# w_down of a hybrid decoder layer in fp32: which output columns use seven products, and in what order ScalarE serves them

## What is computed

```
h = rmsnorm(x, ffn_norm)
gate, up = h @ w_gate, h @ w_up          # 2048 x 5632 each
x = x + (silu(gate) * up) @ w_down       # 5632 x 2048
out = rmsnorm(x, final_norm)
```

## Time and profile before

| | us |
|---|---|
| median of 3 runs (lowest, highest) | 1979.58 (1979.37, 1979.76) |
| span of the profiled execution | 1977.3 |
| its own time, one of the above, so | 2.1 to 2.5 above the span |
| TensorE busy | 1967.3 (99%) |
| VectorE busy | 1654.7 (84%) |
| ScalarE busy | 1126.6 (57%) |
| POOL busy | 167.2 (8%) |
| HBM read | 242.99 MB |

### The profile page before, as it was taken

One profiled execution on the slowest core, in us unless ns is written; L12 is line 12 of the kernel. 1 busy time (PEld: TensorE's weight loads), 2 busy tenths in 40 slices (PEclk: granted clock), 3 DMA queues, 4 the chain that ended last, 5 costly groups with the idle time before them and its releaser, 6 DMA issues.

```text
span 1977.3 us, 29282 instructions
## 1 busy us (share of the span) xinstructions
PE 1967.3 (99%) x10300; PEld 1691.6 (86%) x10300; DVE 1654.7 (84%) x2386; ACT 1126.6 (57%) x2064; POOL 167.2 (8%) x261
## 2 busy tenths in 40 slices
PE   9999999999999999999999999999999999999998
PEld 7888888888888988888888888888888888888886
DVE  8877767777766999999999999999998688697886
ACT  6566666666346655555646555555556355566643
POOL 5002333223100000000000000000000000000000
PEclk9999999999999999999999999999999999999999
DMA  9322222224334344443434344444347836546433
GB/s 343 127 83 70 70 71 70 69 70 139 102 117 138 119 148 137 130 139 130 137 132 142 131 134 135 136 139 135 132 138 238 303 120 227 176 148 221 126 130 133
DMA packets 132889, 276.16 MB, mean 140 GB/s; under 512 B 13392, under 2 KB 13424, under 8 KB 131744
## 3 DMA queue, kind: packets, MB, share of 16 engines
q1 hardware_dynamic: 120896, 239.65, 37.9%
q0 software_dynamic: 6640, 23.82, 3.1%
q10 hardware_dynamic: 5232, 11.04, 1.6%
HBM read 242.99 MB, written 31.46 MB: 139 GB/s over the span
## 4 chain that ended last, share of the span: by engine, by line
PE 96%; DVE 2%; issue 1%; DMA 1%; ACT 0%; SPq 0%; POOLq 0%; POOL 0%; DVEq 0%; ACTq 0%
PE bank L841 25%; PE bank L844 13%; PE bank L702 7%; PE bank L768 7%; PE bank L770 7%; PE bank L769 7%; PE bank L704 7%; PE bank L703 7%; PE bank L900 3%; PE bank L898 3%; PE bank L899 3%; PE bank L925 2%; PE bank L942 1%; PE bank L910 1%; PE bank L909 1%
## 5 line engine op out<-in xcount | busy, mean ns | idle before, releaser
L841 PE MATMUL bank<-s_two,t_hi 128*128 128x512 f32 x2352 | 557.3, 390 | 0.0
L1485 ACT ACTIVATE t_hi<-t_raw 128x1792 fp32r<-128x1792 f32 x176 | 302.5, 1720 | 358.1 <-DVE t_raw L2155 269.7
L841 PEld LDWEIGHTS bank<-s_two,t_hi 128*128 128x128 f32 x2352 | 433.5, 188 | 84.7
L2161 DVE TENSOR_TENSOR t_lo<-t_raw,t_hi 128x1792 fp32r<-128x1792 f32 x176 | 355.7, 2021 | 20.7 <-ACT t_hi L1485 20.6
L844 PEld LDWEIGHTS bank<-s_two,t_lo 128*128 128x128 f32 x2352 | 298.9, 191 | 10.4 <-DVE t_lo L2161 0.6
L844 PE MATMUL bank<-s_two,t_lo 128*128 128x256 f32 x2352 | 302.1, 283 | 0.4 <-DVE t_lo L2161 0.4
L1136 ACT ACTIVATE w_hi<-raw 128x512 fp32r<-128x512 f32 x268 | 168.8, 631 | 189.5 <-PE bank L770 141.4
L1778 DVE TENSOR_TENSOR w_lo<-raw,w_hi 128x512 fp32r<-128x512 f32 x268 | 184.6, 690 | 56.6 <-ACT w_hi L1136 56.0
L2152 DVE TENSOR_TENSOR t_raw<-t_raw 128x1024 f32<-128x1024 f32 x176 | 215.0, 1221 | 17.2 <-DMA t_raw<-in_w_gu 15.5
L702 PE MATMUL bank<-h_hi,w_hi 128*128 128x512 f32 x416 | 166.0, 399 | 1.1 <-DVE h_lo L1782 0.6
L704 PE MATMUL bank<-h_lo,w_hi 128*128 128x512 f32 x416 | 162.6, 391 | 0.0
(11 more groups left out here) (260 smaller groups left out, 3487.8 us busy)
## 6 DMA issues: line engine op xcount, KB each, us to landing
t_raw<-in_w_gu SPq DMA_DIRECT2D x348, 256.0 KB, 2.8
raw<-in_w_down SPq DMA_DIRECT2D x112, 256.0 KB, 3.6
raw<-in_w_in SPq DMA_DIRECT2D x104, 256.0 KB, 2.7
gu_mid<-part POOLq DMA_DIRECT2D x43, 512.0 KB, 2.9
gu_next<-gu_mid SPq DMA_DIRECT2D x36, 512.0 KB, 6.9
raw<-in_w_out SPq DMA_DIRECT2D x64, 256.0 KB, 3.0
fast_y<-in_w_down SPq DMA_DIRECT2D x24, 512.0 KB, 5.0
fast_z<-in_w_down SPq DMA_DIRECT2D x16, 512.0 KB, 4.7
```

The source lines that it names most:

```text
L841: mm = nc.tensor.matmul(b[:, :], t_hi[r][:, ti, q, :], both, start=d == 0 and q == 0, stop=d == DOUBLES - 1 and q == 1 and i < 4, skip_gro ...
L1485: nc.scalar.activation(t_hi[r][:, :, :, :].rearrange("p a q c -> p (a q c)"), t_raw[r][:, 1:8, :, :].rearrange("p a q c -> p (a q c)"), AC ...
L2161: nc.vector.tensor_tensor(t_lo[r][:, :, :, :].rearrange("p a q c -> p (a q c)"), t_raw[r][:, 1:8, :, :].rearrange("p a q c -> p (a q c)"), ...
```

## The change

- The order of down: first 8 tiles plain for all four columns (`plain_unit`: 16 units of two tiles, 24 matmuls each), then four chunks of 8 tiles with seven products for **all four** columns, then the last 4 tiles plain in both position halves.
- A fast unit is (c, p, u, h): chunk, product, half u of the rows (two tiles), and h, which of the two column pairs (0 with 2, 1 with 3); 12 matmuls. The activation sums of (c, p, u) serve both h. 28 units per chunk, 112 in all.
- The plain sums of the first 8 tiles are copied to m_sum (`keep_plain`) in the places of P2, P4, P3 and P5, and seeded into PSUM with the first chunk; the rest units of positions 0 to 255 go on accumulating in the banks of P2 and P3. The residual is added only at the end (`add_block`, `add_last`); the products are joined (`join`) during the last chunk.
- The ring of converted weights (f_hi, f_lo) has four buffers instead of two, the ring of activations four instead of three. Slot v runs at unit v: VectorE makes the sum of unit v+4 and the low part of unit v+3, ScalarE the high part of unit v+3. In a slot ScalarE comes to f_high and a_high first, then to keep and seed, then to silu.
- Far gate tiles (k = 4 to 7) are double buffered, near ones (0 to 3) are not. Gate work has fixed slots (GATE_SLOT).
- At the start of down, the conversions stand ahead of `take_products(7, 1, 0, 4)`, and the first loads wait for `t_used`.

```diff
-FAST_U = 2 * FAST
-FAST_SUMS = 8
-FAST_FROM = "xxyzyxz"
-FAST_BANK = ((0, 4), (6, 1))
-P5, P6, P7, P3, P1, P4, P2 = range(FAST)
-SLOTS = (("S", 0), ("S", 1), ("P", 0), ("S", 2), ("P", 1), ("S", 3), ("P", 2), ("S", 4), ("P", 3), ("S", 5),
-         ("P", 4), ("S", 6), ("P", 5), ("S", 7), ("P", 6), ("S", 8), ("P", 7), ("S", 9), ("S", 10), ("P", 8),
-         ("S", 11), ("P", 9), ("S", 12), ("P", 10), ("S", 13), ("P", 11), ("P", 12), ("P", 13), ("P", 14), ("P", 15))
...
+P1, P5, P7, P6, P4, P3, P2 = range(FAST)
+SUMMED_W, SUMMED_A = (P5, P7, P6, P4), (P5, P7, P6, P3)
+FAST_FROM = "yyxyyzx"
+FAST_BANK = (((0, 4), (6, 1)), ((2, 3), (5, 7)))
+CHUNKS = 4
+ENDING = CHUNKS - 1
+PLAIN, REST = -1, CHUNKS
+BLOCKS, REST_BLOCKS = 16, 8
+F_RING, A_RING = 4, 4
+F_AHEAD, SUM_AHEAD = 3, 4
...
+UNITS = [(PLAIN, n, u, 0) for n in range(NC) for u in range(4)] + [(c, p, u, h) for c in range(CHUNKS) for p in range(FAST) for u in range(2) for h in range(2)]
+UNIT_AT = {unit: v for v, unit in enumerate(UNITS)}
+ITEMS = [(c, p, u) for c in range(CHUNKS) for p in range(FAST) for u in range(2)]
...
+GATE_SLOT = {4: 4, 5: 6, 6: 8, 7: 10, 0: 14, 1: 16, 2: 18, 3: 20}
+PLAIN_SLOT = {4: 4, 5: 5, 6: 6, 7: 7, 0: 8, 1: 9, 2: 10, 3: 11}
...
+        for v in range(BLOCKS, len(UNITS)):
+            c, p, u, h = UNITS[v]
+            e = v - FIRST_UNIT[c]
+            if p == P7:
+                sp.wait_ge(f_lo_done, v + 1)
+                load_block("x", c, u, h, 1, 0)
+            if p == P4:
+                sp.wait_ge(f_lo_done, v + 1)
+                if c < ENDING:
+                    load_block("y", c + 1, u, h, 0, 0)
+                else:
+                    load_rest("y", u, h)
+            if p == P3:
+                sp.wait_ge(f_lo_done, v + 1)
+                if c < ENDING:
+                    load_block("z", c + 1, u, h, 1, 1)
+                else:
+                    load_rest("z", u, h)
+            if p == P2:
+                sp.wait_ge(f_lo_done, v + 1)
...
+            if p == P1:
+                sp.wait_ge(gs_done, GATE[c, 3])
+                if c > 0:
+                    sp.wait_ge(a_lo_done, ITEM[c - 1, P2, 1] + 1)
+                else:
+                    sp.wait_ge(act_lo_done, 16 + 4)
+                load_gu(c + 1, 4 + e)
+            if p == P6 and h == 1:
+                sp.wait_ge(a_sum_done, A_SUM[c, P6, u])
+                if c < ENDING:
+                    for k in (2 * u, 2 * u + 1):
+                        load_gu(c + 1, k)
...
+        def fast_unit(v):
+            c, p, u, h = UNITS[v]
+            pe.wait_ge(f_lo_done, v + 1)
+            pe.wait_ge(a_lo_done, ITEM[c, p, u] + 1)
+            if u == 0 and (c, p, h) in SEED:
+                pe.wait_ge(seeded, seeded_count(c, p, h))
+            elif u == 0 and p == P1:
+                pe.wait_ge(kept, 8 + 2 * (h + 1))
             elif u == 0:
...
+                pe.wait_ge(kept, kept_count(c, p - 2, h))
+            rf, ra = v % F_RING, ITEM[c, p, u] % A_RING
+            for tp in range(2):
+                for i in range(2):
+                    ah, al = a_hi[ra][:, i, P * tp:P * (tp + 1)], a_lo[ra][:, i, P * tp:P * (tp + 1)]
...
+        def rest_unit(q, t, bank_used, first):
+            u, ts = q % 2, slice(P * t, P * (t + 1))
             for i in range(2):
...
+        for v in range(BLOCKS):
+            plain_unit(v).then_inc(f_used, 1)
+        for v in range(BLOCKS, len(UNITS)):
+            fast_unit(v).then_inc(f_used, 1)
+        pe.wait_ge(act_lo_done, 16 + 6)
+        for i, n in enumerate(REST_COLS):
+            for u in range(2):
+                pe.wait_ge(f_lo_done, len(UNITS) + 2 * i + u + 1)
+                for t in range(2):
+                    mm = rest_unit(2 * i + u, t, last_bank(2 * i + t), False)
+                    if u == 1:
                         mm.then_inc(last_ready, 1)
+        for m in range(8, 16):
+            t, n = LAST[m]
+            pe.wait_ge(grp_taken, TAKEN_MIX + m - 7)
+            for u in range(2):
+                mm = rest_unit(2 * REST_COLS.index(n) + u, t, last_bank(m), True)
+            mm.then_inc(last_ready, 1)
...
+        def keep(c, p, h):
+            act.wait_ge(f_used, UNIT_AT[c, p, 1, h] + 1)
+            if (c, p) == (0, P5):
+                act.wait_ge(joined, h + 1)
+            for tp in range(2):
+                nc.scalar.activation(m_sum[p][h][:, tp, :], bank_of(c, p, h, tp)[:, :], ACT.Copy).then_inc(kept, 1)
+        def seed(c, p, h):
+            if c > 0:
+                act.wait_ge(kept, kept_count(*two_before(c, p), h))
+            elif p == P5:
+                act.wait_ge(kept, 16)
             else:
...
+                act.wait_ge(kept, kept_count(0, p - 2, h))
+            if (c, p) == (0, P3):
+                act.wait_ge(joined, h + 1)
             for tp in range(2):
...
+                nc.scalar.activation(bank_of(c, p, h, tp)[:, :], m_sum[p][h][:, tp, :], ACT.Copy).then_inc(seeded, 1)
+        def two_before(c, p):
+            return (c, p - 2) if p > 1 else (c - 1, p - 2 + FAST)
+        def fast_slot(v):
+            c = UNITS[v][0]
+            e = v if c == PLAIN else v - FIRST_UNIT[c]
+            if v in (4, 8, 12, 16):
+                keep_plain(v // 4 - 1)
+            if v == 16:
+                for h in range(2):
+                    seed(0, P5, h)
+            if v == 0:
+                d_high(2)
+                silu(PLAIN, 6)
+                silu(PLAIN, 7)
+            if v == 1:
+                d_high(3)
+            if v + F_AHEAD < len(UNITS):
+                f_high(v + F_AHEAD)
+                for item in items_at(v + F_AHEAD):
+                    a_high(item)
+            else:
+                last_pair(v + F_AHEAD - len(UNITS))
+            for cd, p, h in finished_at(v - 1) if v > 0 else []:
+                if cd < ENDING or p < P3:
+                    keep(cd, p, h)
+                    c2, p2 = two_later(cd, p)
+                    if (c2, p2, h) in SEED:
+                        seed(c2, p2, h)
+            for k, slot in (PLAIN_SLOT if c == PLAIN else GATE_SLOT).items():
+                if e == slot + 1 and (c + 1, k) in GATE:
+                    silu(c + 1, k)
+            if (c, e) in ((ENDING, 22), (ENDING, 23)):
+                r_high(e - 22)
+            if (c, e) == (ENDING, 26):
+                act.wait_ge(act_lo_done, 16 + 6)
+                act.dma_start(g_fin[:, :], final_norm.partition_broadcast(P)).then_inc(gfin_loaded, 16)
...
+        silu(PLAIN, 0)
+        silu(PLAIN, 1)
         act.wait_ge(t_used, ALL_T - 2)
-        silu(0, 0)
-        silu(0, 1)
-        split(U_DOWN // 4, 0)
-        down_high(0, 0)
-        split(U_DOWN // 4, 1)
-        down_high(0, 1)
-        split(U_DOWN // 4, 2)
-        take_products(7, 1, 0, 5)
-        silu(0, 2)
-        take_products(7, 1, 5, QUAD)
-        silu(0, 3)
-        down_first()
-        for c in range(1, CHUNKS):
-            down(c)
+        f_high(0)
+        d_high(0)
+        f_high(1)
+        silu(PLAIN, 2)
+        silu(PLAIN, 3)
+        take_products(7, 1, 0, 4)
+        act.wait_ge(t_used, ALL_T)
+        d_high(1)
+        f_high(2)
+        take_products(7, 1, 4, QUAD)
+        silu(PLAIN, 4)
+        silu(PLAIN, 5)
...
+        def join(p, q, h, needed, op=ALU.add, dst=None):
+            dve.wait_ge(joined, needed)
+            nc.vector.tensor_tensor(flat(m_sum[p if dst is None else dst][h]), flat(m_sum[p][h]), flat(m_sum[q][h]), op).then_inc(joined, 1)
+        def add_block(src, half, n, scale, needed):
+            dve.wait_ge(added, needed)
             for tp in range(2):
                 t = tp + 2 * half
...
+                xt = x_res[t][:, 512 * n:512 * (n + 1)]
+                nc.vector.scalar_tensor_tensor(xt, src[tp], scale[:, t:t + 1], xt, ALU.mult, ALU.add).then_inc(added, 1)
+        def sum_of(p, h):
+            return [m_sum[p][h][:, tp, :] for tp in range(2)]
+        def ending(e):
+            if e == 16:
+                for t in range(2):
+                    dve.wait_ge(x_moved[t], X_BACK)
+                dve.wait_ge(kept, kept_count(ENDING, P1, 1))
+                for h in range(2):
+                    add_block(sum_of(P1, h), 0, h, r2_sign, 0)
+            if e == 18:
+                dve.wait_ge(kept, kept_count(ENDING, P6, 1))
+                for h in range(2):
+                    join(P6, P1, h, 0)
+            if e == 19:
+                for h in range(2):
+                    join(P7, P6, h, 3 + h)
+            if e == 20:
+                for h in range(2):
+                    join(P6, P5, h, 3 + h)
+            if e == 21:
+                for h in range(2):
+                    join(P5, P7, h, 5 + h)
+            if e == 24:
+                dve.wait_ge(kept, kept_count(ENDING, P4, 1))
+                for h in range(2):
+                    join(P7, P4, h, 5 + h, ALU.subtract, P4)
+            if e == 26:
+                for h in range(2):
+                    dve.wait_ge(joined, 7 + h)
```

(98 more changed lines are left out.)

786 lines of the change are left out of this document (277 added, 509 removed).

## The result

The changed kernel takes **1983.1 us** (median of 15 runs, 1981.82 to 1984.04), the kernel before in the same session 1979.45 (15 runs, 1978.42 to 1980.79). The ratio is 1.0018, 95% interval 1.001 to 1.0025: 0.18% slower, where the forecast was 1981.1, 2.0 us lower. The sign is clear of noise; the size is just inside the 4 us that the prediction called no change. The profiled execution spans 1979.7 us, and its own time is 1981.82, the lowest of the 15. The median of before had moved by 0.1.

The account below looks back on a forecast made before the run. TensorE bounds the kernel, and helpers falling behind make it wait. Terms -21.8 + 2.5 + 7.8 + 6.4 + 2.6 + 4.0 = +1.5 us bring span 1977.3 to 1978.8, so median 1981.1 us; range 1972 to 1992.

Parts of the forecast that it names:

- Removed matmuls: In down, 2016 matmuls become 1920; 96 x 0.2267 = 21.8 us less on TensorE.
- VectorE in a steady chunk: In down's chunks 1 and 2, unit 19's low half comes late: 3.2 us per chunk, 6.4 in both, period 79.4.
- rival 3: VectorE's row durations count, not its steps: 18 us more in heavy stretches, 2 at the end, 2001 us; 5 in 100.
- rival 4: VectorE does its sums in light slots, so chunks 1 to 3 lose nothing: 9.0 us less, 1972 us; 18 in 100.
- Chunk 0: First chunk of down: copies and seeds stand ahead of the conversion, and unit 19 is 7.8 us late.
- Chunk 3: Last chunk of down: lateness peaks at 2.6 us, then TensorE waits 4.0 us during VectorE's end work.
- Rival 1: Down's conversions fall out of step: ScalarE's keep and seed delay f_hi, VectorE stands still; 17 us, 1998 us; 12 in 100.
- The way in: At the start of down, the first product's bank is freed late and the fourth unit waits: 2.5 us, ends 0 and 5.
- Rival 2: Start of down later than worked out, from w_down and gu landings or a late bank: +4 to +6, 1986 us; 18 in 100.
- From span to median: Whole kernel: 2.3 us between profiled span 1977.3 and median 1979.58, carried over from 1978.8 to 1981.1 us.
- Seeding costs TensorE nothing: In down's chunks, a seed is done over two units before its first matmul, so it costs nothing.
- HBM traffic: In a chunk of down, SP's loads are 12.6 MB in 79 us, 159 GB/s against 182 before: no cost.

## Why the prediction was right, and where it wasn't

The forecast was right in its mechanism and in the size of its main terms. One term was too small, and part of that error was hidden by luck.

- **Removed matmuls**: -21.8 us. The pace of 0.2267 us holds to the fourth digit; the step is right. (The last matmul before the change begins at 1969.47; the 1969.2 that the prediction names, the last of line 703, would give 0.2266.)
- **VectorE in a steady chunk**: 79.38, twice, against 79.4 worked out. The low half of unit 19 was due at 54.8 us into the chunk; it comes at 1740.44 + 1.14 - 1687.08 = 54.5. This refutes rival 3 (durations instead of steps, chunks of 84) and rival 4 (the lead carries, chunks of 76.2). The run with the gates moved shows what rival 4 would have needed.
- **Chunk 0**: 7.8 worked out, 7.85 measured. With its order repaired 5.5 was expected to be left, and 5.57 was.
- **Chunk 3**: 2.6 + 4.0 = 6.6 worked out, 6.47 measured, with the same shape (largest wait 1.34, where 1.4 was stepped through).
- **Rival 1**, out of step: not in this kernel. In the heavy slots it is the other way round, and VectorE's pauses on f_hi lie in the light slots, where they cost nothing. The whole price of the other order is 2.8 us by the medians and 3.7 by the chunks of the traces, where rival 1 had 17.
- **The way in** is the term that was mis-sized. "I take 2.5 us" was a value between 0.8 + 1.1 and that plus 1.5 for gate tiles landing behind w_down's blocks; measured were 2.6 us of standing still and 1.33 in the plain units, 3.9. Of these 0.56 don't show in the span, because the stages ahead ended that much earlier in the profiled execution: that is luck. The late landing of a gate tile (8.6 us against the 6.9 used) had been priced at 1.5, of which the 2.5 takes in 0.6. The run with the copies ahead of silu 2 and 3 goes from the last product to the first down matmul in 0.12 us, as before the change: what held TensorE was the bank, freed late because its copy stood behind a silu that waited for the gate tile, and not w_down's blocks. Rival 2 had this cause at 4 to 6 us; it is real, at 1.4 above the 2.5.
- **From span to median** there were 2.3 us before and 3.4 now (1983.1 - 1979.7), since the profiled execution was the fastest of the 15. That is 1.1 of the 2.0 us by which the forecast fell short, the start 0.9. Each of the 15 runs lasted 2.0 to 2.2 us longer than its own span, so the difference lies inside the spans. Two causes can be read in part. The stages ahead of down ended early in the profiled execution: their last matmul begins at 1511.97, in the ten experiments' traces between 1511.59 and 1513.25, six times at 1512.7 or later. And 11 of the 15 runs had a mean granted clock of 0.998 (median 1983.20), where the profiled one and three more had 0.999 (1982.36). The trace of the run with copies first, also at 0.998, has such a place: after TensorE stood still for 2.45 us at 1512.5 the window 1516 to 1520 has a granted clock of 0.57, and its plain units lose 1.71 us instead of 1.33. How much of the 1.1 is due to each stays open.
- **"Seeding costs TensorE nothing"** is right for the bank it fills (no wait on a seed), but seeds cost 6.0 us in all by the medians by way of ScalarE's queue, 1.1 of them in each steady chunk, at one place. The ledger had it inside the terms, without saying so.
- **HBM traffic**: the prediction read 182 GB/s in the earlier trace rows, which show 179. Nothing hangs on it; the changed kernel's steady chunk has the 159 worked out.

## What to carry to other kernels

When each helper's total is below the bound, add up its work over the stretch that the ring's lead can bridge, not over the whole loop: here 73 of 76 us was enough to keep TensorE waiting 3.2 us a chunk, and moving work that isn't urgent to where the helper rests gave it back (with the start, the ends and the order, 1983.1 became 1960.5). Ask for every reordering which operation starts the tight stretch, and what stands before that one; the same order that gained 2.8 us in the tight kernel lost 1.2 in the loose one. And before moving work to an idle engine, look at whether the two can run together at all.
